# Attention kernel: one transposed tile moves to the scores' PSUM banks, gate tiles alternate between two banks, and gate products wait for their sums one by one

## The chip, the core and the metric

The kernel runs on one core of one Trainium2 chip. The metric is the device time of one execution in microseconds (us); the median of several executions is compared. In the profile PE is TensorE, DVE is VectorE, ACT is ScalarE, POOL is GpSimd and SP is SyncE, which issues the DMAs.

## The reference, cut to what matters

The first block mixes a sequence of 512 rows by two linear-attention mixers and merges them under gates. The part that matters here is the second mixer's gate, `sigmoid(mg + b_gate)`: one 1024 x 1024 matmul on the 512 rows. Then come two hybrid layers. Each computes, for four blocks of 128 queries, causal attention of four kinds: selected keys ("slc"), window ("win"), latent ("mla") and a short window of 128 keys ("swa"), and a small attention on compressed keys, whose result is added to the same output as slc and win:

```
p_c = softmax(where(valid_c, lc, NEG)) * valid_c        # 128 queries x 4 heads x up to 31 compressed keys
o_cmp = einsum(p_c, vc)
o = g0 * o_cmp + g1 * o_slc + g2 * o_win
mixed = concatenate([o, o_b, o_c]) * silu(z)            # z = h @ w_in[..., ZC:], the layer's output gate
x = x + rms_norm(mixed @ w_out, g_post)
```

## The kernel before

Every engine has its own program, written in the order in which it runs; semaphores join them. Each engine counts what it has finished; a name such as `nt["g7", p, k]` or `ng["gS", p]` is the count to wait for, and a later count covers all earlier ones. A wait for a count that was already waited for is left out.

**PSUM.** There are eight banks of 512 columns. `ps.take(t, name, bank=b)` lets PE wait until whoever read the bank's last tile is done (`ps.empty`). Without `bank` the banks go round.

**The second mixer's gate** (`yb_t`, `seven_gates_t`). The 1024 x 1024 matmul is cut in four parts p; each is done by seven half-size products, in the manner of Strassen, instead of eight. Their operands are sums of blocks: POOL makes four sums of weights for each p (`seven_sums_g`, line 1900), DVE makes four sums of rows once (`seven_sums_v`, line 1890). One product is four matmuls of 256 columns in the program and eight records in the profile (every float32 matmul of the program shows as two). PE takes the tiles (p, k) in the order (0,0), (1,0), (0,1), (0,2), (0,3), (1,1), ... `G7` says which products a tile holds: k=0 products 1 and 2, which need no sum; k=1 products 6 and 7; k=2 products 5 and 3; k=3 product 4. Ahead of every k>0 PE waits for all four sums of weights of that p and all four sums of rows.

**Attention** (`attn_t`). The 40 jobs (ten per block of queries, each a kind and two heads, e=0 and 1) run through a pipeline: in round i PE makes the scores of job i, transposes the weights of job i-4 (`turn`, line 2688), and multiplies job i-6 by the values (`product`). DVE adds the bias and finds the least score (`least`, line 2794); ACT exponentiates (line 2916); DVE takes reciprocals (line 2800); POOL scales (lines 2973 and 2975); PE transposes; DVE (line 2781) and ACT (line 2926) share the copies out of PSUM. In even rounds PE goes transposes, gate, scores, products; in odd rounds products, scores, gate, transposes. DVE's copy of a transposed tile stands behind `least` of the same round in odd rounds.

Banks: scores go round `rings[0]`, transposed tiles round `rings[1]`. Until round 12 (`few`) these are banks (0,1) and (3,4), and banks 2 and 5 hold the tiles of the layer's output gate; later (`all_`) they are (2,0,1) and (5,3,4). In round 5 of each block of queries `turn_cmp` transposes the compressed weights (line 2697) into a bank of `rings[1]`, and DVE copies it (line 2822).

**The output gate** z (`out_gate`): six of its eight tiles m are spread over rounds 0 to 11, four matmuls of 512 columns per round, in the order 5, 4, 0, 1, 2, 3, in bank `(2, 5)[m % 2]`. When a tile is full ACT takes its tanh (line 2438) and DVE multiplies it (line 2433), which empties the bank.

Of the kernel before, what the change touches and what calls it, by code (L numbers as in the profile page):

```python
# [8 lines left out]
ALU = mybir.AluOpType  # L9
# [103 lines left out]
def program(nc, I, out):  # L113
# [3 lines left out]
    sv, sa, sg, st = (nc.alloc_semaphore(f"{e}_finished") for e in ("vector", "scalar", "gpsimd", "tensor"))  # L117
    nv, na, ng, nt = Count(), Count(), Count(), Count()
# [25 lines left out]
    ps = Banks(nc.alloc_psum_tensor("PS", [128, 4096], F32))  # L144

    def mm(t, o, l, r, s, p):
        return t.matmul(o, l, r, start=s, stop=p, skip_group_check=True)  # L147
# [27 lines left out]
    def weights(t, k):  # L175

        t.wait_ge(s_ring[ring_slot(k)], 16 * sum(wparts(i) for i in range(k + 1) if ring_slot(i) == ring_slot(k)))
        return wviews(k)
# [1630 lines left out]
    def yb_t(t):  # L1809
        meet(t, "delta")  # L1810
        seven_gates_t(t)
        t.wait_ge(sv, nv["y", "b"])
        for h in range(4):
            p = ps.take(t, "yT", "b", h)
            for a in range(4):
                for c in range(2):
                    x = t.go.transpose(p[:, 128 * a + 64 * c:128 * a + 64 * c + 64],
                                       sqB[rows(h), 512 * a + 256 * (h // 2) + 128 * c:512 * a + 256 * (h // 2) + 128 * c + 128],
                                       ident[rows(h), rows(h)])
            x.then_inc(st, nt("yT", "b", h))  # L1820
        nt.mark("at", "yb")

    def yb_v(v):
        meet(v, "delta")
        seven_sums_v(v)
        head_norm_v(v, oB, sqB, s4B, "b")
        nv.mark("y", "b")
        for p in range(4):
            seven_gates_v(v, p)
        for h in range(4):  # L1830
            v.wait_ge(sa, na["bg", h])
            v.wait_ge(st, nt["yT", "b", h])
            v.do.scalar_tensor_tensor(out=ybT[:, h, :], in0=ps["yT", "b", h][:, :], scalar=vc("gon"), in1=gateB[h],
                                      op0=ALU.mult, op1=ALU.mult).then_inc(sv, nv("ybT", h))
            ps.empty(sv, nv, "yT", "b", h)
        nv.mark("at", "yb")
# [15 lines left out]
    def yb_g(g):  # L1852
        meet(g, "delta")
        for p in range(2):
            seven_sums_g(g, p)
        rsq_g(g, s4B, "heads", "b")
        for p in range(2, 4):
            seven_sums_g(g, p)
        ng.mark("at", "yb")
# [15 lines left out]
    T1g, T2g, T4g = (AR[:, VT_at + 1024 * i:VT_at + 1024 * i + 1024].rearrange("p (k n) -> p k n", k=4) for i in range(3))  # L1875
# [3 lines left out]
    he, hf, hg, hh = (hT[:, 4 * (i // 2):4 * (i // 2) + 4, 256 * (i % 2):256 * (i % 2) + 256] for i in range(4))  # L1879

    def gate_blocks(w, p):
        return [w[:, 4 * (i % 2):4 * (i % 2) + 4, 256 * (p % 2) + 128 * (i // 2):256 * (p % 2) + 128 * (i // 2) + 128] for i in range(4)]

    def gate_sums(p):
        return [AR[:, ST_at[p % 3] + 512 * i:ST_at[p % 3] + 512 * i + 512].rearrange("p (k n) -> p k n", k=4) for i in range(3)]

    def seven_sums_v(v):

        for o, x, y in ((T1g, hf, he), (T2g, hh, T1g), (hf, hh, hf), (T4g, hg, T2g)):
            v.do.tensor_tensor(o, x, y, ALU.subtract).then_inc(sv, nv("gT"))  # L1890

    def seven_sums_g(g, p):

        w, = weights(g, 13 + 2 * (p // 2))
        a, b, c, d = gate_blocks(w, p)
        s1, s2, s4_ = gate_sums(p)
        if p == 3:
            g.wait_ge(st, nt["g7", 0, 3])
        for o, x, y, op in ((s1, c, d, ALU.add), (s2, s1, a, ALU.subtract), (c, a, c, ALU.subtract), (s4_, b, s2, ALU.subtract)):
            g.do.tensor_tensor(o, x, y, op).then_inc(sg, ng("gS", p))  # L1900


    G7 = ((1, 2), (6, 7), (5, 3), (4,))

    def seven_gates_t(t):
        for p, k in [(0, 0), (1, 0)] + [(p, k) for p in range(2) for k in range(1, 4)] + [(p, k) for p in range(2, 4) for k in range(4)]:
            w, = weights(t, 13 + 2 * (p // 2))
            a, b, c, d = gate_blocks(w, p)
            s1, s2, s4_ = gate_sums(p)
            if k:  # L1910
                t.wait_ge(sg, ng["gS", p])
                t.wait_ge(sv, nv["gT"])
            o = ps.take(t, "g7", p, k)
            for i, what in enumerate(G7[k]):
                left, right = {1: (a, he), 2: (b, hg), 3: (s4_, hh), 4: (d, T4g), 5: (s1, T1g), 6: (s2, T2g), 7: (c, hf)}[what]
                for q in range(4):
                    x = mm(t.go, o[:, 256 * i:256 * i + 256], left[:, q, :], right[:, q, :], q == 0, q == 3)
            x.then_inc(st, nt("g7", p, k))
            if p % 2 and k == 3:
                nt.mark("weights", 13 + 2 * (p // 2))  # L1920
# [390 lines left out]
    def two_t(t, l):  # L2311
# [95 lines left out]
        for i in range(8):  # L2407
            out_gate(t, l, 7, i)
# [6 lines left out]
        for i in range(8):  # L2415
            out_gate(t, l, 6, i)

    def out_gate(t, l, m, i, bank=None):

        k = W2 + 10 * l + 7 - m // 4  # L2420
        w, = weights(t, k)
        if i == 0:
            ps.take(t, "sz", l, m, bank=bank)
        x = mm(t.go, ps["sz", l, m][:, :], w[:, i, 128 * (m % 4):128 * (m % 4) + 128], hT2[:, i, :], i == 0, i == 7)
        if i == 7:
            x.then_inc(st, nt("sz", l, m))
            if m in (4, 3):
                nt.mark("weights", k)

    def out_gate_v(v, l, m):  # L2430
# [170 lines left out]
    NJ, PER = len(JOBS), 10  # L2601
    TURN, PV = 4, 6
    CMP_EXP, CMP_SUM, CMP_TURN, CMP_PV = 1, 2, 5, {1: 0, 4: 1}
    GATES = [(m, i) for m in (5, 4, 0, 1, 2, 3) for i in range(8)]
    PER_JOB = 4
    FILLED = len(GATES) // PER_JOB

    def gates_in(i):

        x = GATES[PER_JOB * i:PER_JOB * i + PER_JOB]  # L2610
        return x, [m for m, k in x if k == 7]
# [39 lines left out]
    def attn_t(t, l):  # L2651
# [41 lines left out]

        def turn_cmp(qb):
            t.wait_ge(sg, ng["pc", l, qb])
            p = ps.take(t, "pcT", l, qb, bank=next(rings[1]))
            t.go.transpose(p[:, 0:128], Pc.rearrange("p h c -> p (h c)"), ident).then_inc(st, nt("pcT", l, qb))

        def product(j):
# [24 lines left out]
        def turned(i):  # L2724
            qb, at = divmod(i, PER)
            if TURN <= i < NJ + TURN:
                turn(i - TURN)
            if qb < 4 and at == CMP_TURN:
                turn_cmp(qb)
# [15 lines left out]
        def filled(i):  # L2745
            for m, k in gates_in(i)[0]:
                out_gate(t, l, m, k, bank=(2, 5)[m % 2])

        for i in range(NJ + PV):
            rings = few if i <= FILLED else all_  # L2750
# [377 lines left out]
```

## Time and profile before

| | |
|---|---|
| median of 3 runs | 1378.41 us (1377.52 to 1380.28) |
| the profiled execution | 1377.88 us, of which 1376.1 us span |
| PE busy | 1310.5 us, 95% |
| DVE, ACT, POOL busy | 46%, 30%, 26% |
| gate of the second mixer | 600 to 651 us |
| attention of the two layers | 865 to 1003 us, 1180 to 1318 us |

The span runs from the first instruction to the last; about 1.8 us of the execution lie around it. A timeline row is: start, duration, engine, line, operation, shapes, number of records merged, and in brackets the idle time of the engine just before the row and what ended it.

### The profile page before, as it was taken

The numbers are of one execution on the slowest core, as the hardware profiler recorded it, in microseconds if no ns is written. First come the engines' busy times: TensorE is split into PE (matmuls) and PEld (weight loads), VectorE is DVE, ScalarE is ACT, GpSimd is POOL, SyncE is SP. The second block draws the span as 40 slices with busy tenths as digits, with TensorE's granted clock in tenths as the row PEclk, the third lists the DMA queues.
The fourth block names the chain that finished last, engine by engine and source line by source line (L and its number), as shares of the span: only waits on it lengthen the run. The fifth ranks groups of instructions, "written<-read, shape, count | busy, mean of one in ns | idle before, by whom it ended". The sixth has DMA issues, their size and how long they took to land.

```text
span 1376.1 us, 23425 instructions
## 1 busy us (share of the span) xinstructions
PE 1310.5 (95%) x9443; PEld 763.7 (55%) x9443; DVE 637.9 (46%) x1350; ACT 416.8 (30%) x901; POOL 354.6 (26%) x437
## 2 busy tenths in 40 slices
PE   5999989999999999999999999998999999998897
PEld 3454654555566677668445645445655645445553
DVE  4266627747233344464464222237636131327735
ACT  4233303353432222201015112236613212236621
POOL 0100000112323443153430000127631000117631
PEclk9999999999999999999999999999999999999999
DMA  9611012011220100032244315110003515100001
GB/s 318 251 61 62 2 63 77 8 53 62 77 110 3 64 2 3 3 122 75 100 158 105 117 31 184 62 50 1 2 16 74 148 31 183 62 1 1 1 1 61
DMA packets 71530, 96.52 MB, mean 70 GB/s; under 512 B 27639, under 2 KB 35247, under 8 KB 71422
## 3 DMA queue, kind: packets, MB, share of 16 engines
q1 hardware_dynamic: 71050, 94.76, 20.5%
q8 instruction: 74, 1.21, 0.4%
q10 hardware_dynamic: 372, 0.27, 0.1%
q14 instruction: 34, 0.28, 0.1%
HBM read 92.89 MB, written 2.13 MB: 69 GB/s over the span
## 4 chain that ended last, share of the span: by engine, by line
PE 85%; DVE 7%; ACT 2%; issue 2%; SPq 2%; POOL 1%; DMA 1%; DVEq 0%; POOLq 0%; ACTq 0%
PE PS L147 82%; PE PS L2688 2%; DVE AR L2794 2%; DMA AR<-in_w_mod 1%; SPq L187 1%; DVE AR L2781 1%; POOL AR L1900 1%; ACT AR L2916 1%; DVE AR L2045 0%; PE PS L1383 0%; SPq L304 0%; PE PS L2103 0%; DVE AR L819 0%; ACT AR L2926 0%; DVE AR L2830 0%
## 5 line engine op out<-in xcount | busy, mean ns | idle before, releaser
L147 PE MATMUL PS<-AR 64*64 64x64 f32 (+14 forms) x8806 | 1236.5, 337 | 36.8 <-ACT AR L2926 6.6
L147 PEld LDWEIGHTS PS<-AR 64*64 64x64 f32 (+5 forms) x8806 | 694.0, 155 | 551.3 <-issue 462.5
L2916 ACT ACTIVATE AR<-AR 128x257 f32<-128x257 f32 (+5 forms) x160 | 84.9, 530 | 104.8 <-DVE AR L2794 95.5
L2794 DVE CUSTOM_DVE_ANT_0 AR<-PS,AR 128x257 f32<-128x257 f32 (+5 forms) x160 | 72.3, 452 | 67.1 <-PE PS L147 50.0
L412 POOL TENSOR_TENSOR AR<-AR 128x1 f32<-128x1 f32 (+4 forms) x26 | 21.8, 840 | 280.4 <-DVE AR L407 233.6
L1175 DVE SCALAR_TENSOR_TENSOR AR<-AR 128x441 f32<-128x441 f32 (+2 forms) x96 | 78.6, 819 | 19.6 <-ACT AR L1132 15.9
L1557 DVE TENSOR_TENSOR AR<-PS,AR 128x256 f32<-128x256 f32 x60 | 25.5, 425 | 100.7 <-PE PS L147 97.7
L2975 POOL TENSOR_SCALAR AR<-AR 128x257 f32<-128x257 f32 (+5 forms) x96 | 53.4, 556 | 62.2 <-DVE AR L2800 54.8
L2688 PE MATMUL PS<-AR 128*128 128x128 f32 x352 | 51.2, 283 | 8.4 <-DVE AR L2781 6.3
L1684 ACT ACTIVATE AR<-PS 128x512 f32<-128x512 f32 x48 | 28.7, 598 | 92.5 <-PE PS L147 90.0
L2973 POOL TENSOR_SCALAR AR<-AR 128x128 f32<-128x128 f32 (+3 forms) x64 | 38.9, 608 | 66.5 <-DVE AR L2800 61.7
L1992 POOL TENSOR_TENSOR AR<-AR 128x512 f32<-128x512 f32 x36 | 47.5, 1319 | 31.4 <-DMA AR<-in_w_o 28.4
L2688 PEld LDWEIGHTS PS<-AR 128*128 128x128 f32 x352 | 39.0, 143 | 29.4 <-issue 14.1
L2045 DVE TENSOR_TENSOR AR<-PS,AR 128x512 f32<-128x512 f32 x40 | 27.7, 692 | 52.4 <-PE PS L147 50.7
L1792 POOL TENSOR_TENSOR AR<-AR 128x512 f32<-128x512 f32 x20 | 21.0, 1050 | 84.2 <-PE PS L147 55.6
L2926 ACT ACTIVATE AR<-PS 128x512 f32<-128x512 f32 (+2 forms) x56 | 30.1, 537 | 28.6 <-PE PS L2688 24.7
L2433 DVE SCALAR_TENSOR_TENSOR AR<-AR,PS 128x512 f32<-128x512 f32 x16 | 11.0, 688 | 52.1 <-ACT AR L2438 52.0
L2781 DVE COPY AR<-PS 128x512 f32<-128x512 f32 (+2 forms) x48 | 28.9, 602 | 7.9 <-PE PS L2688 6.4
L2983 POOL TENSOR_TENSOR AR<-AR 128x28 f32<-128x28 f32 (+3 forms) x8 | 2.5, 315 | 112.3 <-DVE AR L2810 111.8
L2000 POOL TENSOR_TENSOR AR<-AR 128x512 f32<-128x512 f32 x12 | 16.9, 1407 | 55.0 <-PE PS L147 54.3
L1195 POOL TENSOR_TENSOR AR<-AR 128x512 f32<-128x512 f32 (+1 forms) x12 | 12.9, 1071 | 68.5 <-ACT AR L1141 50.3
L1900 POOL TENSOR_TENSOR AR<-AR 128x512 f32<-128x512 f32 x16 | 27.2, 1700 | 11.4 <-DVE AR L1627 10.1
(260 smaller groups left out, 880.5 us busy)
## 6 DMA issues: line engine op xcount, KB each, us to landing
AR<-in_w_in SPq DMA_DIRECT2D x16, 2048.0 KB, 8.8
AR<-in_w_mod SPq DMA_DIRECT2D x6, 2048.0 KB, 12.8
AR<-in_w_out SPq DMA_DIRECT2D x4, 2048.0 KB, 12.9
AR<-in_x SPq DMA_DIRECT2D x8, 512.0 KB, 5.9
AR<-in_w_in SPq DMA_DIRECT2D x4, 1024.0 KB, 7.8
AR<-in_w_o SPq DMA_DIRECT2D x2, 2048.0 KB, 8.5
AR<-in_w_in SPq DMA_DIRECT2D x2, 1664.0 KB, 9.4
AR<-in_w_in SPq DMA_DIRECT2D x12, 256.0 KB, 4.8
```

Source lines behind the costliest of these rows:

```text
L147: return t.matmul(o, l, r, start=s, stop=p, skip_group_check=True)
L1175: v.do.scalar_tensor_tensor(out=o_, in0=xi[:, r0 + i - 1:r1 + i - 1, c0 + c - 1:c1 + c - 1], scalar=tap(i, c), in1=o_, op0=ALU.mult, op1=A ...
L1684: a_.do.activation(XX[n], ps.two("xx", n, k_, k)[:, new_at(k):new_at(k) + 512], ACT.Copy, bias=0.0, scale=1.0).then_inc(sa, na("xx", n, k_ ...
L1900: g.do.tensor_tensor(o, x, y, op).then_inc(sg, ng("gS", p))
L1992: g.do.tensor_tensor(o, x, y, ALU.subtract).then_inc(sg, ng(*name, "T"))
L2688: x = t.go.transpose(p[:, c + 128 * b:c + 128 * b + 128], PB[j % NJP][e][:, at[b]:at[b] + 128], ident)
L2781: write(dst, src).then_inc(sem, count("pT", l, j, e))
L2794: v.do.tensor_tensor_reduce(PB[j % NJP][e][:, 0:nk], ps["s", l, j, e][:, 0:nk], bias_for(qb, kind, 2 * a + e, nk), 1.0, 3e38, ALU.add, ALU ...
L2916: a_.do.activation(P, P, ACT.Exp, bias=mn[:, j % NJS, e:e + 1], scale=-1.0, accum_out=su[:, j % NJS, e:e + 1]).then_inc(sa, na("p", l, j, e))
L2926: out_of_psum(a_, sa, na, lambda o, x: a_.do.activation(o, x, ACT.Copy, bias=0.0, scale=1.0), l, i - TURN, e)
L2973: x = g.do.tensor_scalar(P, P, r, gt_[:, qb, c:c + 1], ALU.mult, ALU.mult)
L2975: x = g.do.tensor_scalar(P, P, r, one_c, ALU.mult, ALU.mult)
```

## The change

Three edits. (1) In the second mixer's gate each product waits for the one sum that it reads (`G7_S`, `G7_T`), no longer for all eight. (2) The output gate's tiles go in the order 5, 4, 1, 0, 3, 2, so that neighbouring tiles have different banks; the release of the weights' ring slot moves to the tile that is now last. (3) For blocks of queries 1 to 3 the transposed compressed weights take a bank of the scores' ring; the ring of the transposed tiles is not advanced there, so the tile after it gets the bank one place earlier in that ring, and the scores after it one place later in theirs.

```diff
     def seven_sums_v(v):
-        for o, x, y in ((T1g, hf, he), (T2g, hh, T1g), (hf, hh, hf), (T4g, hg, T2g)):
-            v.do.tensor_tensor(o, x, y, ALU.subtract).then_inc(sv, nv("gT"))
+        for i, o, x, y in ((1, T1g, hf, he), (2, T2g, hh, T1g), (3, hf, hh, hf), (4, T4g, hg, T2g)):
+            v.do.tensor_tensor(o, x, y, ALU.subtract).then_inc(sv, nv("gT", i))
...
-            g.do.tensor_tensor(o, x, y, op).then_inc(sg, ng("gS", p))
+            g.do.tensor_tensor(o, x, y, op).then_inc(sg, ng("gS", p, i))
...
+    G7_S, G7_T = {5: 1, 6: 2, 7: 3, 3: 4}, {5: 1, 6: 2, 7: 3, 3: 3, 4: 4}
...
-            if k:
-                t.wait_ge(sg, ng["gS", p])
-                t.wait_ge(sv, nv["gT"])
             o = ps.take(t, "g7", p, k)
             for i, what in enumerate(G7[k]):
+                if what in G7_S:
+                    t.wait_ge(sg, ng["gS", p, G7_S[what]])
+                if what in G7_T:
+                    t.wait_ge(sv, nv["gT", G7_T[what]])
...
-            if m in (4, 3):
+            if m in (4, 2):
                 nt.mark("weights", k)
...
-    GATES = [(m, i) for m in (5, 4, 0, 1, 2, 3) for i in range(8)]
+    GATES = [(m, i) for m in (5, 4, 1, 0, 3, 2) for i in range(8)]
...
-            p = ps.take(t, "pcT", l, qb, bank=next(rings[1]))
+            p = ps.take(t, "pcT", l, qb, bank=next(rings[0] if qb else rings[1]))
```

No instruction is added or removed, and the orders of DVE, ACT, POOL and SP stay as they were; only PE's waits change. In the pieces below, "vector_finished" is a wait for DVE, "gpsimd_finished" for POOL, "scalar_finished" for ACT, "ring..._landed" for a DMA of weights.

PE in the second mixer's gate; the row with x15 ends the tiles (0,0) and (1,0), and the row after it opens (0,1):

```order
 L147 MATMUL PS<-AR 128x256 x15
 L147 MATMUL PS<-AR 128x256 [waits vector_finished,gpsimd_finished]
-L147 MATMUL PS<-AR 128x256 x19
+L147 MATMUL PS<-AR 128x256 x3
+L147 MATMUL PS<-AR 128x256 [waits vector_finished,gpsimd_finished]
+L147 MATMUL PS<-AR 128x256 x7
 L147 MATMUL PS<-AR 128x256 [waits gpsimd_finished]
-L147 MATMUL PS<-AR 128x256 x19
+L147 MATMUL PS<-AR 128x256 x3
+L147 MATMUL PS<-AR 128x256 [waits vector_finished]
```

The one wait ahead of twenty matmuls became waits ahead of single products. Over the whole stage, from (0,1) to the last product, 7 matmuls with a wait became 16.

PE in round 4 of a layer's attention: two transposes of job 0, four matmuls of the third gate tile (128x512), then the scores of job 4 (128x128, two rows):

```order
-L2688 MATMUL PS<-AR 128x128 [waits gpsimd_finished] x2
-L147 MATMUL PS<-AR 128x512 [waits vector_finished,ring1_landed]
-L147 MATMUL PS<-AR 128x512 x3
-L147 MATMUL PS<-AR 128x128 x2
+L2691 MATMUL PS<-AR 128x128 [waits gpsimd_finished] x2
+L147 MATMUL PS<-AR 128x512 [waits ring1_landed]
+L147 MATMUL PS<-AR 128x512 x3
+L147 MATMUL PS<-AR 128x128 [waits vector_finished] x2
```

The gate tile lost its wait for DVE; the scores of job 4 now show a wait for DVE of their own, which the gate tile's had covered.

PE in rounds 35 and 36, last block of queries: the compressed weights (first row, line 2697, 2700 after), the four transposes of job 32, the two scores of job 36 (128x512):

```order
-L2697 MATMUL PS<-AR 128x128 [waits scalar_finished,gpsimd_finished]
-L2688 MATMUL PS<-AR 128x128 [waits vector_finished]
-L2688 MATMUL PS<-AR 128x128 x3
-L147 MATMUL PS<-AR 128x512 x2
+L2700 MATMUL PS<-AR 128x128 [waits vector_finished,gpsimd_finished]
+L2691 MATMUL PS<-AR 128x128 [waits scalar_finished]
+L2691 MATMUL PS<-AR 128x128 x3
+L147 MATMUL PS<-AR 128x512 [waits vector_finished] x2
```

The transposes wait for ACT in place of DVE, and the compressed weights and the scores have a wait for DVE that they lacked. Round 25 and 26 (third block) change in the same way. In the second block the compressed weights and the first score after them gain a wait for DVE, and nothing is lost.

## Rows read from the trace of the kernel before

**Rows 1.** The page, part 1: busy time, share of the span, instructions of each engine.

```profile
PE 1310.5 (95%) x9443; PEld 763.7 (55%) x9443; DVE 637.9 (46%) x1350; ACT 416.8 (30%) x901; POOL 354.6 (26%) x437
```

**Rows 2.** Timeline, 596 to 634 us, the second mixer's gate.

```profile
600.11 7.68 DVE L1890 TENSOR_TENSOR AR<-AR 128x1024 f32<-128x1024 f32 x4
...
600.13 7.18 PE L147 MATMUL PS<-AR 128*128 128x256 f32 x32 [0.79 <-DVE AR L1627]
600.16 15.91 POOL L1900 TENSOR_TENSOR AR<-AR 128x512 f32<-128x512 f32 x8 [10.13 <-DVE AR L1627]
...
608.97 25.36 PE L147 MATMUL PS<-AR 128*128 128x256 f32 x116 [1.65 <-POOL AR L1900]
...
619.25 12.46 POOL L1900 TENSOR_TENSOR AR<-AR 128x512 f32<-128x512 f32 x8
621.57 6.88 DVE L1925 TENSOR_TENSOR AR<-PS,AR 128x256 f32<-128x256 f32 x14
```

**Rows 3.** Critical chain, 590 to 665 us: start, duration, what; POOL's third and fourth sum.

```profile
604.58 2.14 POOL AR L1900
...
606.79 2.13 POOL AR L1900
```

**Rows 4.** DVE's line 1890: min/median/max in ns, first and last start in us.

```profile
L1890 DVE TENSOR_TENSOR AR<-AR x4: 1226/2086/2179, 600.1 to 605.6; 128x1024 f32<-128x1024 f32 x4
```

**Rows 5.** Groups by line and form, PE, 617 to 619 us: count, busy us, mean ns, idle.

```profile
L147 PE MATMUL PS<-AR 128*128 128x256 f32 x11 | 2.5, 378 | 0.0
```

**Rows 6.** Four windows of line 147, 608.97 to 650.70 us: total length, then PE busy.

```profile
sum 41.73, PE 41.73 PEld 36.18; mean PE 10.43 PEld 9.04
```

**Rows 7.** Timeline, 876 to 894 us: round 4 of the first layer.

```profile
881.27 0.69 DVE L2433 SCALAR_TENSOR_TENSOR AR<-AR,PS 128x512 f32<-128x512 f32 x1 [2.79 <-ACT AR L2438]
...
882.11 4.10 PE L147 MATMUL PS<-AR 128*128 128x512 f32 x12 [1.28 <-DVE AR L2433]
```

**Rows 8.** Timeline of PE, second layer, round 4.

```profile
1197.03 4.10 PE L147 MATMUL PS<-AR 128*128 128x512 f32 x12 [1.28 <-DVE AR L2433]
```

**Rows 9.** Timeline, first layer, rounds 25 to 27.

```profile
955.28 0.43 DVE L2794 CUSTOM_DVE_ANT_0 AR<-PS,AR 128x257 f32<-128x257 f32 x1
...
956.36 0.66 PE L2688 MATMUL PS<-AR 128*128 128x128 f32 x4 [0.28 <-DVE AR L2781]
...
960.86 0.42 DVE L2794 CUSTOM_DVE_ANT_0 AR<-PS,AR 128x257 f32<-128x257 f32 x1 [0.75 <-PE PS L147]
```

**Rows 10.** Timelines of PE and of DVE, second layer, rounds 26 and 27.

```profile
1271.62 0.66 PE L2688 MATMUL PS<-AR 128*128 128x128 f32 x4 [0.62 <-DVE AR L2781]
...
1276.13 0.42 DVE L2794 CUSTOM_DVE_ANT_0 AR<-PS,AR 128x257 f32<-128x257 f32 x1 [0.76 <-PE PS L147]
```

**Rows 11.** Timeline, first layer, rounds 35 to 37.

```profile
983.40 0.42 DVE L2794 CUSTOM_DVE_ANT_0 AR<-PS,AR 128x257 f32<-128x257 f32 x1
...
983.87 0.69 DVE L2781 COPY AR<-PS 128x512 f32<-128x512 f32 x1
...
984.61 0.66 PE L2688 MATMUL PS<-AR 128*128 128x128 f32 x4 [1.59 <-DVE AR L2781]
984.66 0.29 DVE L2822 COPY AR<-PS 128x128 f32<-128x128 f32 x1
...
985.11 4.85 PE L147 MATMUL PS<-AR 96*128 96x512 f32 x42
...
989.99 0.42 DVE L2794 CUSTOM_DVE_ANT_0 AR<-PS,AR 128x257 f32<-128x257 f32 x1 [1.35 <-PE PS L147]
```

**Rows 12.** Timelines of PE and of DVE, second layer, rounds 36 and 37.

```profile
1299.88 0.66 PE L2688 MATMUL PS<-AR 128*128 128x128 f32 x4 [1.60 <-DVE AR L2781]
...
1305.26 0.42 DVE L2794 CUSTOM_DVE_ANT_0 AR<-PS,AR 128x257 f32<-128x257 f32 x1 [1.30 <-PE PS L147]
```

**Rows 13.** Timeline of POOL, first layer, round 13 on.

```profile
926.07 1.21 POOL L2973 TENSOR_SCALAR AR<-AR 128x256 f32<-128x256 f32 x2 [5.65 <-DVE AR L2800]
```

**Rows 14.** Windows of 5 us: busy by engine, granted clock, DMA share, GB/s.

```profile
930.00:935.00 5.00, 5.00 (x34) 3.88 (x32) 4.05 (x14) 2.52 (x9) 3.14 (x5) 0.73 0.00 0
```

More of the change, by code:

```diff
@@ L1898, in seven_sums_g @@
             g.wait_ge(st, nt["g7", 0, 3])
-        for o, x, y, op in ((s1, c, d, ALU.add), (s2, s1, a, ALU.subtract), (c, a, c, ALU.subtract), (s4_, b, s2, ALU.subtract)):
-            g.do.tensor_tensor(o, x, y, op).then_inc(sg, ng("gS", p))
+        for i, o, x, y, op in ((1, s1, c, d, ALU.add), (2, s2, s1, a, ALU.subtract), (3, c, a, c, ALU.subtract), (4, s4_, b, s2, ALU.subtract)):
+            g.do.tensor_tensor(o, x, y, op).then_inc(sg, ng("gS", p, i))
     G7 = ((1, 2), (6, 7), (5, 3), (4,))
+    G7_S, G7_T = {5: 1, 6: 2, 7: 3, 3: 4}, {5: 1, 6: 2, 7: 3, 3: 3, 4: 4}
     def seven_gates_t(t):
```

## The prediction

> **What bounds the kernel now.** I read the page first: PE is busy for 1310.5 of 1376.1 us [rows 1], so time can only come from the 65 us in which PE idles, or from work taken off it; the change takes none off. Then I read the timeline at the three places that the diff touches, looking at the bracket ahead of each PE row: how long PE stood, and which line let it go. Last I looked at what DVE and POOL did at the same moment, since a stall that goes is worth only what the next engine in the chain can follow.
>
> **Gate of the second mixer.** PE makes the tiles (0,0) and (1,0) from 600.13 to 607.31, stands for 1.65 us and goes on at 608.97, released by POOL's line 1900 [rows 2]. The chain shows why: POOL's fourth sum runs from 606.79 to 608.92 [rows 3], and PE waits for all four. Product 6, the next one, reads only the second sum of each kind. POOL's was done when its third began at 604.58 [rows 3]. DVE's four end at 607.79 [rows 2], and none takes less than 1.226 us [rows 4], so its second was done by 605.34. So product 6 can start at 607.31.
>
> The later products must not be early. PE's 116 records take 25.36 us, 0.219 us each [rows 2], so a product of eight takes 1.75 us. Product 7 is due at 609.06; POOL's third sum is done at 606.72 [rows 3] and all of DVE's at 607.79. Product 3 is due at 612.56, its sum is there at 608.92. The tile (1,1) is due at 616.06, and by 616.07 POOL has done all eight sums of the first two parts [rows 2]; it needs the sixth. The third part starts at 624.8: its bank was emptied by DVE's first line 1925, which begins at 621.57, and its second sum is needed at 628.3, while POOL runs the last eight sums from 619.25 to 631.71 [rows 2], 1.56 us each, so it is there near 622.4. The last part needs sums from 640.5 on. No new stall, then.
>
> What a stall costs is more than its bracket: in a row without idle time records last 0.378 us [rows 5] and follow each other every 0.219 us, so they overlap by 0.16 us, which a stall loses. Term: 1.65 + 0.16 = 1.81 us. I take the same 0.16 us for the other places (an estimate from these rows).
>
> The price of the waits themselves: 9 more matmuls carry one. The seven before cost nothing that can be seen: in 41.73 us that hold six of them PE is busy for 41.73 us [rows 6]. So I take zero. If each emptied PE's overlap, the bound is 9 x 0.16 = 1.44 us. The Trainium skill (Advanced Engine Details and Errata, Network/Comms) puts reading a semaphore from a sequencer at 50 to 100 ns; nine such reads in PE's path would be an estimated 0.45 to 0.9 us, and the sum below would be 7.8 to 7.3 us in place of 8.2. The trace disagrees for the waits that it has, if they are met in time.
>
> **Output gate.** In round 4 of each layer PE stands for 1.28 us [rows 7, 8], because tile 0 wants bank 2, which tile 4 has just filled and DVE's line 2433 empties from 881.27 to 881.96 [rows 7]. With tile 1 next the bank is 5, whose last tile was finished two rounds earlier. The scores behind it wait for `least` of round 3, which stands ahead of line 2433 on DVE, so that is no new stall. Tiles 0, 3 and 2 then find a bank that was filled two rounds before, as tiles 1 to 3 did until now. Does the gain last? POOL idles for 5.65 us until 926.07 [rows 13] waiting for DVE, and DVE's least score waits for PE, so all engines move with PE. Term: 2 x (1.28 + 0.16) = 2.88 us. Bounds: 0 if a later wait takes it, 2.88 us.
>
> **Compressed weights.** The transposes of job 22 wait 0.28 us in the first layer [rows 9] and 0.62 in the second [rows 10], those of job 32 wait 1.59 [rows 11] and 1.60 [rows 12], all for DVE's copy (line 2781) of the tile that had their bank, which on DVE stands behind `least` of the same round. With the shorter ring order they want a bank that ACT emptied a round before; that stall goes. What is late next? The scores of job 36 now need both banks of job 35's. Without the stall the transposes start at 983.02 and the scores at 983.5 (985.11 - 1.59) [rows 11]. `least` leaves the second bank at 983.82 [rows 11], and the second score comes one score later, at 984.4 (512 columns, twice the 0.44 us that 256 take [rows 2]): 0.5 us to spare. The first bank is free earlier still. In round 26 the scores start at 956.6 and the later bank is free at 955.71 [rows 9]. So nothing new on PE. But DVE does not move: it runs through from the copy at 983.87 and next waits for PE, 1.35 us before 989.99 [rows 11] and 1.30 before 1305.26 [rows 12]. That idle time is all that it can give, less 0.10, the distance that DVE keeps when PE is long done (983.87 + 0.69 to 984.66) [rows 11]. The same cap in the second layer's round 27 is 0.76 - 0.10 [rows 10]; in the first layer 0.75 [rows 9] does not bind. Terms: 0.28 + 0.16 = 0.44; 0.66; 1.25; 1.20. Together 3.55 us. Bounds: 0 if each goes into the next wait; without DVE's cap 0.44 + 0.78 + 1.75 + 1.76 = 4.73.
>
> In the second block the added wait is for scores two places back; I take zero, bounded by one wait of the size of 0.28 us in each layer.
>
> **Sum.** 1.81 + 2.88 + 3.55 = 8.24 us. Against the profiled execution, 1377.88, that is 1369.6; the median of the runs is 0.53 above that execution, so I forecast 1370.2, 0.6% faster. A measurement of this kernel tells about 0.2% (2.8 us) from no change.
>
> **Rivals**, on the scale of the median.
>
> *The compressed weights' gain goes into the next wait* (3.55 us lost): 1373.7. For it: DVE has no idle time until 988.6. Against: the 1.35 us right behind.
>
> *The added waits cost PE its overlap*: 1.44 us, 1371.6.
>
> *TensorE's clock falls once or twice more.* In 930 to 935 us the granted clock is 0.73 of full speed [rows 14], so 1.2 GHz for 2.7 of these 5 us and 2.4 GHz for the rest, after short stalls and small matmuls; that loses 1.35 us of full-speed work. Twice where PE is the bound: 1372.9. For it: the stretches are full of short matmuls and short waits, and the change moves where they fall. Against: it takes idle time out. The Trainium skill (TensorE: Matmul & The Clock Gate, A second HAM failure mode) says that going round PSUM banks with small idle gaps between groups of matmuls lets the clock fall again and again; by that rule alternating banks would lose what the waits gave. The trace bears it out at one place in the two layers' attention [rows 14].
>
> *The scores' ring runs short; slower.* Each of the six transposes of compressed weights (three blocks, two layers) takes one of three score banks until DVE's copy. If PE reached the scores before DVE had emptied the banks, each place would cost the old stall plus that copy: 1.59 + 0.10 + 0.29 = 1.98 us [rows 11], 11.9 in all. Against it stand 4.69 us from the two gates and the four stalls removed, 4.09: 3.1 us slower, 1381.5. It decides when the spare 0.5 us above is gone. That bank is held for about one round and `least` precedes the copy on DVE, so I hold it unlikely.
>
> *The waits do not fall away*, because another release comes just as late: 1378.4. Each bracket names the releaser, and the three found are those that the diff removes.
>
> **Chances.** Forecast 0.68; next wait 0.12; added waits 0.06; clock 0.08; ring short 0.03; nothing 0.03. The first four are faster by more than 0.2%: 0.94, of which I give 0.02 to what I have not seen: faster 0.92, same 0.05, slower 0.03. The range reaches down to the sum without DVE's cap (9.42 us, 1369.0) and 1.8 us under it for the spread of the runs, and up to the case 1373.7 with 0.5 added: 1367.2 to 1374.2.
>
> **What will show it.** Right: no bracket of POOL's line 1900 ahead of PE near 607 us; none of line 2433 in round 4; none of line 2781 ahead of the transposes right after line 2697; the idle time of DVE in rounds 27 and 37 near its minimum; the first three gains still there at the span's end. Wrong: brackets of DVE's line 2794 or 2822 ahead of the scores of rounds 16, 17, 26, 27, 36 and 37, gaps at each waiting product in the gate, or new windows with a clock under 1.

## The result, and the profile after

The changed kernel takes 1369.78 us (median of 4 runs, 1369.23 to 1372.44) where the kernel before takes 1378.51 (4 runs, 1377.52 to 1380.28): a ratio of 0.9941, with a 95% interval of 0.9925 to 0.9957. Measured once more beside other runs of before, it was 1371.12 against 1379.76, 0.9938 (0.9924 to 0.9952). The forecast was 1370.2, so 0.9940.

The changed kernel's lines stand three further down in its file from the gate on (line 2794 is 2797, 2781 is 2784, 2688 is 2691, 2697 is 2700). Its page begins:

```profile
span 1370.6 us, 23430 instructions
...
PE 1312.6 (96%) x9443; PEld 766.5 (56%) x9443; DVE 636.6 (46%) x1350; ACT 416.5 (30%) x901; POOL 354.8 (26%) x437
```

The span is 5.5 us shorter, the median 8.7. The difference is time that this execution lost before it came to anything that was changed: it reached the gate at 603.11 us, the kernel before at 600.13 [rows 2]. So I compare stretches. These are the windows of the gate, from its first matmul to the transposes behind it, of the changed kernel and then of the kernel before (length, PE busy, weight loads, DVE, ACT, POOL, granted clock, DMA share, GB/s):

```profile
603.11:651.75 48.64, 48.64 (x225) 42.22 (x225) 27.01 (x35) 6.12 (x11) 30.13 (x17) 1.00 0.33 123
```
```profile
600.13:650.70 50.57, 48.91 (x225) 42.15 (x225) 27.02 (x35) 6.12 (x11) 30.11 (x17) 1.00 0.31 118
```

PE now has no idle time in the gate, and the stretch is 1.93 us shorter: the idle 1.65 us [rows 2], and 0.27 us by which PE is busy longer with the same records (48.91 against 48.64), because the stall breaks their overlap. The timeline of round 4 in the first layer of the changed kernel, on PE (the bracket is the idle time ahead of a row and the line that ended it; where a row has none, PE did not stand):

```profile
881.50 0.38 PE L2691 MATMUL PS<-AR 128*128 128x128 f32 x2
881.72 4.03 PE L147 MATMUL PS<-AR 128*128 128x512 f32 x12
886.13 4.14 PE L147 MATMUL PS<-AR 64*128 64x129 f32 x11 [0.39 <-DVE AR L2797]
```

The bracket of 1.28 us [rows 7] is gone, and the scores of round 5 come 4.63 us after round 4's transposes; in the kernel before these are at 880.44 and 886.59, 6.15 apart. The gain is 1.52 us, and 1.51 in the second layer, where the bracket is gone as well. The timeline of rounds 36 and 37 in the first layer, PE and then DVE:

```profile
981.79 0.27 PE L2700 MATMUL PS<-AR 128*128 128x128 f32 x1
981.90 0.60 PE L2691 MATMUL PS<-AR 128*128 128x128 f32 x4
982.36 4.96 PE L147 MATMUL PS<-AR 96*128 96x512 f32 x42
...
989.71 0.63 PE L2691 MATMUL PS<-AR 128*128 128x128 f32 x4 [0.93 <-DVE AR L2784]
```
```profile
982.92 0.69 DVE L2784 COPY AR<-PS 128x512 f32<-128x512 f32 x1
983.71 0.29 DVE L2825 COPY AR<-PS 128x128 f32<-128x128 f32 x1
...
987.52 0.17 DVE L2803 RECIPROCAL AR<-AR 128x2 f32<-128x2 f32 x1
987.83 0.42 DVE L2797 CUSTOM_DVE_ANT_0 AR<-PS,AR 128x257 f32<-128x257 f32 x1
```

The transposes no longer wait after the turned weights (1.59 us [rows 11]). By the scores behind them PE has won 1.79 us: they start 0.57 us after the turned weights, where it was 985.11 - 982.75 = 2.36. But 7.35 us after those scores PE stands for 0.93 us, for DVE's copy, where before it stood 0.45 there. What stays is 1.20 us: from the turned weights to those transposes 7.92 us, before 9.12 (982.75 to 991.87). DVE shows why: its wait of 1.35 us [rows 11] has shrunk to the 0.14 us between 987.69 and 987.83, the distance it also keeps ahead of `least` where it does not wait (977.25 to 977.39 in the kernel before). DVE now sets the pace of this place, as the cap in the prediction said. The second layer's rounds 26 and 27 on PE, in the changed kernel:

```profile
1267.00 0.33 PE L2700 MATMUL PS<-AR 128*128 128x128 f32 x1 [0.87 <-POOL AR L2989]
1267.17 0.60 PE L2691 MATMUL PS<-AR 128*128 128x128 f32 x4
...
1273.61 0.52 PE L2691 MATMUL PS<-AR 128*128 128x128 f32 x3 [0.88 <-DVE AR L2784]
```

The 0.62 us [rows 10] are gone. From the turned weights to the bracketed transposes it is 6.61 us, before 7.21 (1270.67 to 1277.88): 0.60 won. The same distance won 0.49 us in the first layer's rounds 26 and 27, and 1.16 in the second layer's 36 and 37.

From the first gate matmul to the end of the last matmul of the program it is 759.85 us (603.11 to 1362.96); in the kernel before, 768.27 (600.13 to 1368.40). That is 8.42 us, and the pieces named above add to 8.41.

### The profile page after: what moved, and what is told of

Same layout as the page of the kernel before. It is cut to its first block, busy times and chain, and to the rows that moved or that the text cites. A ratio compares the mean times of both kernels' runs of the same rounds, so it can differ in the third digit from the quotient of the medians.

```text
span 1370.6 us, 23430 instructions
## 1 busy us (share of the span) xinstructions
PE 1312.6 (96%) x9443; PEld 766.5 (56%) x9443; DVE 636.6 (46%) x1350; ACT 416.5 (30%) x901; POOL 354.8 (26%) x437
## 4 chain that ended last, share of the span: by engine, by line
PE 87%; DVE 5%; POOL 3%; ACT 2%; issue 2%; DMA 1%; ACTq 0%; DVEq 0%; POOLq 0%
PE PS L147 83%; PE PS L2691 2%; POOL AR L2978 1%; DVE AR L2797 1%; POOL AR L1995 1%; ACT AR L2919 1%; DMA AR<-in_onehot 1%; PE PS L353 0%; DVE AR L2048 0%; POOL AR L2976 0%; DVE AR L2784 0%; PE PS L1383 0%; ACT AR L2929 0%; PE PS L2106 0%; DVE AR L819 0%
```

## The experiments

The theory is that of the prediction: each stall is worth its bracket and a little lost overlap, the waits themselves cost nothing, and DVE's idle time caps the compressed weights' gain. The rivals are those of the prediction too. The whole time of one execution is a blunt measure here, since the stretch ahead of the gate, which no kernel changes, ended anywhere from 599.7 to 605.9 us. So each experiment was read by the ratio over its runs and by the stretch from the first gate matmul to the end of the last matmul in its profile:

| kernel | median us | ratio to before (95%) | stretch us | less than 768.27 |
|---|---|---|---|---|
| gate alone | 1378.58 | 0.9992 (0.9978 to 1.0005) | 768.03 | 0.24 |
| tile order alone | 1376.77 | 0.9971 (0.9961 to 0.9981) | 766.87 | 1.40 |
| banks alone | 1377.06 | 0.9973 (0.9965 to 0.9981) | 765.34 | 2.93 |
| turned weights alone | 1376.58 | 0.9970 (0.9957 to 0.9982) | 764.88 | 3.39 |
| changed, 72 more waits | 1371.44 | 0.9940 (0.9927 to 0.9954) | 759.92 | 8.35 |
| changed, bank held | 1373.58 | 0.9961 (0.9948 to 0.9975) | 763.48 | 4.79 |
| changed, copies on ACT | 1368.93 | 0.9925 (0.9912 to 0.9938) | 758.78 | 9.49 |
| changed, POOL earlier | 1368.89 | 0.9925 (0.9912 to 0.9938) | 757.64 | 10.63 |
| changed, both of these | 1366.43 | 0.9905 (0.9888 to 0.9921) | 754.68 | 13.59 |
| changed, again | 1371.12 | 0.9938 (0.9924 to 0.9952) | 759.80 | 8.47 |
| before, again | 1381.19 | one run | 768.36 | -0.09 |

**The gate alone**, on the kernel before: the numbered sums and the waits at each product, nothing else.

```diff
-            if k:
-                t.wait_ge(sg, ng["gS", p])
-                t.wait_ge(sv, nv["gT"])
...
+                if what in G7_S:
+                    t.wait_ge(sg, ng["gS", p, G7_S[what]])
+                if what in G7_T:
+                    t.wait_ge(sv, nv["gT", G7_T[what]])
```

> Only the gate's waits are changed (edit 1), on the kernel before. Theory (three separate local gains): no bracket ahead of PE near the start of the tile (0,1); the stretch from the first gate matmul to the first transpose behind the gate (50.56 us before, 600.13 to 650.70) becomes 48.65 us, 1.9 us shorter, and the time falls by 1.8 to 1.9 us. Rival (added waits cost PE its overlap): only 0.4 us shorter. Rival (a later stage takes it back): the stretch is shorter, the span is not.

Its timeline on PE has the gate in one piece, 605.94 to 654.58, the same 48.64 us as in the changed kernel:

```profile
605.94 48.71 PE L147 MATMUL PS<-AR 128*128 128x256 f32 x224 [0.79 <-DVE AR L1627]
654.58 0.59 PE L1817 MATMUL PS<-AR 64*128 64x64 f32 x7
```

So the edit gives its 1.93 us alone. The whole stretch gained only 0.24, because at another place this execution lost 1.59: the 34 matmuls that begin at 1276.10 took 5.57 us in place of 3.98, at a granted clock that fell. Two of its windows there:

```profile
1276.00:1278.00 2.00, 2.00 (x9) 0.89 (x9) 1.74 (x4) 0.29 (x1) 1.65 (x4) 0.78 0.00 0
1278.00:1280.00 2.00, 2.00 (x22) 2.00 (x22) 1.11 (x5) 1.42 (x4) 1.74 (x2) 0.50 0.00 0
```

Here 0.50 of full speed is 1.2 GHz. The ratio's interval takes in both a gain of 1.9 us (0.9986) and no change; by itself it settles nothing.

**The order of the gate tiles alone**, and **the banks alone**, with the old order, but each tile in the other bank than the tile ahead of it.

```diff
-            if m in (4, 3):
+            if m in (4, 2):
...
-    GATES = [(m, i) for m in (5, 4, 0, 1, 2, 3) for i in range(8)]
+    GATES = [(m, i) for m in (5, 4, 1, 0, 3, 2) for i in range(8)]
```

> Only the order of the output gate's tiles is changed (edit 2), on the kernel before. Theory: the bracket of 1.28 us ahead of the third tile is gone in both layers, the distance from the transposes of round 4 to the scores of round 5 (6.15 us before, 880.44 to 886.59) becomes 4.6 us, and the time falls by 2.9 to 3.0 us. Rival (POOL or DVE is the bound in the next rounds and takes it back): the time falls by less than 1 us.

```diff
-                out_gate(t, l, m, k, bank=(2, 5)[m % 2])
+                out_gate(t, l, m, k, bank=5 if m in (5, 0, 2) else 2)
```

> The order of the tiles stays as before (5, 4, 0, 1, 2, 3); only their banks are made to alternate: 5, 2, 5, 2, 5, 2. Theory (the stall is the bank alone): the same 2.9 to 3.0 us as with the order changed. Rival (it matters which tile and which weights come third): a bracket stays ahead of the third tile and the time falls by under 1 us.

Round 4 in the first layer on PE, with the order changed and then with the banks changed:

```profile
880.66 0.38 PE L2688 MATMUL PS<-AR 128*128 128x128 f32 x2
880.87 4.03 PE L147 MATMUL PS<-AR 128*128 128x512 f32 x12
885.29 4.57 PE L147 MATMUL PS<-AR 64*128 64x129 f32 x12 [0.39 <-DVE AR L2794]
```
```profile
882.51 0.38 PE L2688 MATMUL PS<-AR 128*128 128x128 f32 x2
882.72 4.03 PE L147 MATMUL PS<-AR 128*128 128x512 f32 x12
887.14 4.57 PE L147 MATMUL PS<-AR 64*128 64x129 f32 x12 [0.39 <-DVE AR L2794]
```

Both make it 4.63 us, 1.52 less than before. So the gain is the bank's distance of two rounds and not which tile is made when. The first of the two executions again met the fall of the clock in the second layer (5.59 us for the 34 matmuls); with that 1.61 added its stretch gained 3.01, the other's 2.93.

**The turned weights alone.**

```diff
-            p = ps.take(t, "pcT", l, qb, bank=next(rings[1]))
+            p = ps.take(t, "pcT", l, qb, bank=next(rings[0] if qb else rings[1]))
```

> Only the bank of the transposed compressed weights is changed (edit 3), on the kernel before. Theory: the brackets of line 2781 ahead of the transposes that follow the compressed weights are gone in blocks 3 and 4; DVE's idle time behind falls from 0.75 and 1.35 us to near its minimum; the time falls by 3.3 to 3.6 us. Rival (PE's gain is not capped by DVE): 4.7 us. Rival (the scores' ring runs short): brackets ahead of the scores of rounds 16, 26 and 36, and less than 1 us gained or a loss.

The stretch is 3.39 us shorter. Corrected for the falls of the clock, the three edits alone give 1.83 + 3.01 + 3.39 = 8.23 us; together they gave 8.42. The gains add to within 0.2 us, so none of the three lived off another's stall.

**72 more waits.** In the changed kernel, every matmul of the gate's last three parts waits for a count that POOL reached before the stage began: 88 matmuls of the gate with a wait instead of 16.

```diff
                 for q in range(4):
+                    if p:
+                        t.go.wait_ge(sg, ng["at", "delta"])
                     x = mm(t.go, o[:, 256 * i:256 * i + 256], left[:, q, :], right[:, q, :], q == 0, q == 3)
```

> The changed kernel, with a further wait ahead of each of the 84 matmuls of parts 1 to 3 of the second mixer's gate, for a count that POOL reached before the stage began: 88 matmuls with a wait in place of 16. Theory (a wait that is already met costs PE nothing): the stretch from the first gate matmul to the first transpose behind it stays at 48.6 us. Rival (each costs the 0.16 us of overlap): 72 x 0.16 = 11.5 us longer, 60 us.

Its window of the gate:

```profile
602.29:650.93 48.64, 48.64 (x225) 42.22 (x225) 27.01 (x35) 6.12 (x11) 30.15 (x17) 1.00 0.32 123
```

It is 48.64 us, to the hundredth what it is without them. At 0.16 us each, as in the rival, 72 waits would have made it 60.2. The Trainium skill (Advanced Engine Details and Errata, Network/Comms) gives 50 to 100 ns for a semaphore read; this trace shows nothing of it in PE's path for a wait that is met in time.

**The bank held longer.** In the changed kernel, DVE copies the turned weights out one round later, so that the scores' ring is one bank short for longer. The copy is also what the compressed product reads, two rounds after the turned weights.

```diff
-            if qb < 4 and at == CMP_TURN:
+            if qb < 4 and at == CMP_TURN + 1:
```

> The changed kernel, with DVE's copy of the transposed compressed weights one round later (round 6 of each block in place of round 5), so that the scores' bank is held longer. Theory (the bank came back just in time, with some half a microsecond to spare): the first score two rounds later now waits for that copy, and the kernel loses 0.3 to 1 us at each of six places, 2 to 6 us in all, so most or all of what edit 3 gave. Rival (the scores' ring has ample room): no change within 0.2%.

A wait for line 2825 (2822 of before) appears in every block. Here it is on PE in round 7 and round 37 of the first layer, and in round 37 of the second:

```profile
893.30 4.55 PE L147 MATMUL PS<-AR 128*128 128x128 f32 x14 [0.35 <-DVE AR L2825]
...
985.07 1.12 PE L147 MATMUL PS<-AR 128*128 128x128 f32 x6 [1.14 <-DVE AR L2825]
...
1298.87 1.12 PE L147 MATMUL PS<-AR 128*128 128x128 f32 x6 [1.49 <-DVE AR L2825]
```

It takes back 3.63 us of the stretch, a size that was expected, but not by the expected wait. The bracket stands ahead of the compressed product (`product_cmp`, 128*128), which reads the copy; the scores (64*128) come behind it, at 985.49. In round 7, in the first block, the turned weights keep a bank of the other ring, and the same wait stands there, 0.35 us in both layers. So this run shows what a late copy costs the product that reads it. What a short ring would cost it does not show, since the scores behind would have had to wait for the same copy.

For the ring the changed kernel itself has the answer. No wait for line 2825 stands ahead of PE in its attention, and in blocks 2 to 4 the copy ends 2.1 to 2.9 us before the scores that take its bank (984.00 and 986.61 in the first layer's last block).

**The copies of jobs 22 and 32 on ACT.** If DVE is the cap, taking two copies from it must give back what PE lost 7 us later.

```diff
-        return j % 2 == 0 if e == "both" else e == 0
+        return j % 2 == 0 and j not in (22, 32) if e == "both" else e == 0
```

> The changed kernel, with the copies of jobs 22 and 32 out of PSUM made by ACT in place of DVE (0.69 us each off DVE at the place where DVE, not PE, set the gain). Theory (DVE caps edit 3): the least scores of rounds 36 and 37 come some 0.7 us sooner, the bracket of 0.93 us ahead of the transposes of job 34 falls to 0.4, and the kernel gains 0.4 to 0.6 us at each of the two places of block 4 and up to 0.2 in block 3: about 1.2 us. Rival (DVE is not the cap): no gain, or a loss of up to 0.6 us where ACT becomes late.

The first layer's rounds 36 and 37 on PE:

```profile
981.36 0.27 PE L2700 MATMUL PS<-AR 128*128 128x128 f32 x1
...
988.79 0.63 PE L2691 MATMUL PS<-AR 128*128 128x128 f32 x4 [0.45 <-DVE AR L2784]
```

The distance is 7.43 us against 7.92, and the bracket is back at 0.45. Then PE keeps 1.69 us of the 1.79 that it won, where the cap of the changed kernel left 1.20. The stretch is 1.07 us shorter than the changed kernel's, near the 1.2 expected.

**POOL's order.** The wait ahead of the turned weights, 0.87 us for line 2989 (2986 in the kernel before, where it stands too), is POOL's. In this kernel POOL does another scaling five rounds earlier, and has no sum of weights in round 22: the later sums each come one even round later, the last in round 38.

```diff
-            if i == 15:
+            if i == 10:
                 g.wait_ge(s_pst, 16 * (l + 1))
...
-            if 14 <= i < 38 and i % 2 == 0:
+            if 14 <= i < 40 and i % 2 == 0 and i != 22:
...
-                sums_of_weights(g, w0 + 8, w0 + 9, ("y2", l), (i - 14) // 2)
+                sums_of_weights(g, w0 + 8, w0 + 9, ("y2", l), (i - 14) // 2 - (i > 22))
```

> The changed kernel, with POOL's work moved: the scaling of the 1024-wide norm row (2.78 us) from round 15 to round 10, and the sum of output weights of round 22 to round 38. Theory (PE's brackets for POOL, 0.47, 0.21 and 0.87 us in each layer, are POOL's queue and not its data): these brackets go, and the kernel gains 1 to 3 us in the two layers together; where DVE or ACT is next, less. Rival (another engine bounds those rounds): the brackets change their releaser and nothing is gained.

The first layer's rounds 26 and 27 on PE:

```profile
951.37 0.27 PE L2700 MATMUL PS<-AR 128*128 128x128 f32 x1
...
951.91 4.61 PE L147 MATMUL PS<-AR 96*128 96x384 f32 x34
...
958.64 0.52 PE L2691 MATMUL PS<-AR 128*128 128x128 f32 x3 [0.98 <-DVE AR L2784]
```

The bracket of 0.87 is gone, the stretch 2.21 us shorter than the changed kernel's, although the 34 matmuls took 4.61 us here and 4.69 in the second layer, in place of 3.98; and DVE is late next, 0.98 us.

The longer row is not the clock, which was 1.00 in both (951.91 to 956.52 and 1262 to 1268). Its last four matmuls are the scores of round 27, two for each head. In the repeated changed kernel the two heads' matmuls start together (957.33 and 957.34). Here the second head's start 0.62 us after the first's, and 0.06 us after DVE has finished the first `least` of round 26, in both layers. DVE and then PE in the first layer:

```profile
955.21 0.56 DVE L2797 CUSTOM_DVE_ANT_0 AR<-PS,AR 128x384 f32<-128x384 f32 x1
955.69 0.08 DVE L2797 DVE_READ_ACCUMULATOR2_ANT AR<- 128x1 f32 x1
...
955.83 0.48 PE L147 MATMUL PS<-AR 64*128 64x257 f32 x1
```

So the next bound is DVE here too. No bracket shows it, because PE was busy with the first head's matmuls.

**Both, beside the changed kernel and the kernel before once more.** The diff is that of the last two together.

> The copies of jobs 22 and 32 on ACT together with POOL's earlier scaling and moved sum. From the first turned compressed weights of layer 1 to the last matmul the changed kernel takes 472.21 us, with ACT's copies alone 471.11 (1.10 less), with POOL's order alone 469.77 (2.44 less). Theory: the two remove different waits (DVE's behind line 2784, POOL's ahead of line 2700), so the gains add to 3.5 us or somewhat more, since in the run with POOL's order PE then stood 0.98 us for DVE in round 27, which is the idle time that ACT's copies shorten: a stretch near 468.5, ratio to the kernel before near 0.991. Rival: ACT, which now copies in the rounds in which PE already waits 0.5 to 0.7 us for its line 2929, becomes late, and the gain stays at that of POOL's order: a stretch near 469.8, ratio 0.9925.

> The changed kernel once more, beside the one above and in as many rounds, so that both stand against the same runs of the kernel before: ratio 0.994, within 0.0015. Its profile shows whether the 2.98 us that the first profiled execution was late at the second mixer's gate belong to the change: if they do, the first gate matmul starts near 603.1 again; if they are a matter of the execution (the clock in the first 250 us), anywhere from 598 to 606, and from the first gate matmul to the last matmul of the program it takes 759.9 us again, give or take 1.5.

> The kernel before once more, for one more profile. In the runs of the gate alone and of the tiles alone, which keep the stall of 0.6 us ahead of the transposes after line 2697 in layer 2's round 26, the clock fell right behind it and the 34 matmuls there took 5.6 us in place of 3.98; no profile of a kernel without that stall showed it. If the stall is what lets the clock fall, it can be seen here (in two of four profiles so far); if it is a matter of the execution alone, it says nothing either way, and from the first gate matmul to the last matmul it takes 768.3 us, give or take 1.6.

The three reach the gate at 603.60, 601.31 and 603.34 us. The first rows of the gate of the changed kernel and of the kernel before, both repeated:

```profile
601.31 8.92 PE L147 MATMUL PS<-AR 128*128 128x256 f32 x40 [0.79 <-DVE AR L1627]
```
```profile
603.34 6.97 PE L147 MATMUL PS<-AR 128*128 128x256 f32 x31 [0.79 <-DVE AR L1627]
```

The order has turned round: now the kernel before is the later one, by 2.0 us. So the 2.98 us of the first profile are the execution's and not the change's. The stretches repeat to 0.1 us: 759.80 and 768.36. The kernel before had no fall of the clock behind its stall in the second layer (3.98 us).

Both together take 754.68 us, 5.17 less than the changed kernel, more than the 1.07 and 2.21 alone. From the first turned weights to the last matmul it is 467.1 us, where 468.5 was expected. Of the 1.9 us that the two do not give alone, 1.2 are the scores of round 27, which start together here (the 34 matmuls take 4.00 and 4.08 us): the copy of job 22, which in POOL's run kept DVE 0.69 us ahead of `least`, is ACT's here. Of the other 0.7 us, 0.3 lie ahead of the first layer's attention and 0.4 in rounds 5 to 27. Its ratio of 0.9905 against 0.9938 beside the same runs of before, with intervals that do not touch, makes it the best version: 0.95% under the kernel before.

## Why the prediction was right

**Which stalls fall away, and what bounds.** The signs of "right" are in the trace: no bracket of POOL's sums in the gate, none of the gate copy in round 4, none ahead of the transposes behind the turned weights, DVE's idle time in both rounds 37 and in the second layer's round 27 at its minimum. (In the first layer's round 27, where the cap was not to bind, 0.26 us of it are left.) The gains are still there at the end of the last matmul.

**The terms.** Predicted and measured by distances in the two profiles: gate 1.81 and 1.93; output gate 2.88 and 3.03; compressed weights 0.44, 0.66, 1.25, 1.20 and 0.49, 0.60, 1.20, 1.16. The sum was 8.24, and 8.41 came. Two sizes were a little off. What a stall loses beside its bracket was taken as 0.16 us, from the length and spacing of the records; measured it is 0.28 in the gate (1.93 - 1.65) and 0.24 in round 4 (1.52 - 1.28). Most of the difference is the first matmul behind the stall, shown here with the next two of the kernel before:

```profile
608.97 0.48 PE L147 MATMUL PS<-AR 128*128 128x256 f32 x1 [1.65 <-POOL AR L1900]
609.29 0.60 PE L147 MATMUL PS<-AR 128*128 128x256 f32 x2
```

The next matmul starts 0.32 us after it, where in a row without idle time it is 0.22: 0.10 us that the prediction had not counted. In round 4 the same distance is 0.50 in place of 0.43 us. The other size is DVE's: it kept 0.14 us and not 0.10 where it is the cap. The prediction took the distance between two copies, and the cap stands ahead of `least`.

The two sizes err in opposite ways, 0.27 us too little for the gates and 0.10 too much for the compressed weights, so the sum is nearer than its terms. That the median came within 0.5 us of the forecast is luck in part: the ratio's interval is 4.4 us wide.

**The next wait takes the gain.** It took part of it, 0.59 us of 1.79 in the first layer's last block, exactly where DVE's idle time ran out, and the cap had it in the sum; without the cap the four terms would have been 4.73, and 3.45 came. The copies on ACT show that it is DVE: they take 0.48 us out of that wait.

**The added waits cost overlap.** Refuted by the 72 waits, for waits that are met in time.

**The ring runs short.** One of the signs named for "wrong" did appear, in round 16 of the second layer, where the added wait now holds the scores for line 2797; the same row stands in the first layer of the repeated run. These are PE's rows of the changed kernel:

```profile
1242.22 1.87 PE L147 MATMUL PS<-AR 96*128 96x256 f32 x12 [0.36 <-DVE AR L2797]
1244.25 1.95 PE L147 MATMUL PS<-AR 128*64 128x128 f32 x14 [0.15 <-ACT AR L2929]
```

The kernel before has no wait at the first place and 0.73 us at the second. From the turned weights to the row after these it is 4.97 us (1241.16 to 1246.13) and 4.96 before (1244.83 to 1249.79). The new wait comes out of the one behind it, which had to be waited for in any case. The zero in the sum was right; the sign was not one of harm by itself. The other sign, a wait for the copy of the turned weights, did not appear, so no run shows the 11.9 us that the prediction set on it. In round 36 no margin was left on the first bank, which the prediction took to be free earlier still: the first score starts 0.06 us after `least` has left it (982.30 and 982.36 in the first layer).

**A wait that the prediction did not look for.** The output gate's last tile is now tile 2, in bank 2, which the scores take next; before it was tile 3, in bank 5. So the scores behind the gate tiles wait for line 2436 (2433 before), in both layers, and also with the tile order alone and with the banks alone. PE in the first layer, before and after:

```profile
921.80 1.92 PE L147 MATMUL PS<-AR 64*128 64x257 f32 x14
924.52 0.70 PE L147 MATMUL PS<-AR 64*128 64x256 f32 x2 [0.79 <-DVE AR L2794]
```
```profile
923.02 0.70 PE L147 MATMUL PS<-AR 64*128 64x256 f32 x2 [0.38 <-DVE AR L2436]
924.05 0.70 PE L147 MATMUL PS<-AR 64*128 64x256 f32 x2 [0.34 <-DVE AR L2797]
```

It comes out of the 0.79 us that PE waited there before: from the first turned weights to the second of these two scores it is 33.30 us in both (891.22 to 924.52, 890.75 to 924.05). It costs nothing here, but it was not on the prediction's list.

**The clock falls.** At the place of [rows 14] the changed kernel's window shows a clock of 0.81 in place of 0.73:

```profile
930.00:935.00 5.00, 5.00 (x37) 3.92 (x36) 3.99 (x14) 2.95 (x9) 3.10 (x5) 0.81 0.00 0
```

What it loses there PE doesn't lose at the end: from the first turned weights to those of round 26 it takes 64.54 us (890.75 to 955.29), in the kernel before 64.53, and 64.57 in the repeated kernel before (894.51 to 959.08), whose clock did not fall. PE waits for others right behind it. In the changed kernel's second layer, without a fall, it stands 0.36 and 0.15 us for DVE and ACT in round 16 (the rows above), in the first, with the fall, for neither, and the wait for POOL that comes next ends equally late, 48.86 and 48.87 us after the first turned weights:

```profile
939.61 0.44 PE L2691 MATMUL PS<-AR 128*128 128x128 f32 x2 [0.47 <-POOL AR L2978]
...
1251.33 0.44 PE L2691 MATMUL PS<-AR 128*128 128x128 f32 x2 [0.51 <-POOL AR L2978]
```

Such a fall stands at this place, in one or both layers, in six of the thirteen profiles: the kernel before, the changed one, the turned weights alone, the 72 waits, the copies on ACT and POOL's order. Each began before the turned weights of the second block, the first that edit 3 moves in a layer.

The Trainium skill (TensorE: Matmul & The Clock Gate, A second HAM failure mode) warns of a clock that falls again and again where groups of matmuls go round banks with short idle times between them; the tiles in alternating banks show none of it, and the window 880 to 887 has a clock of 1.00. What remains of this rival is one place, the 34 matmuls behind the turned weights of the second layer's round 26: the clock fell there in two of the thirteen profiles, the gate alone and the tile order alone, both times behind the stall that the change removes. Five profiles have that stall and eight do not, so whether removing it also steadies the clock stays open.

## What to carry to other kernels

A stall on the bound engine is worth its bracket plus a broken overlap and a longer first matmul (here 0.24 to 0.28 us together), but only as far as the idle time of the next engine in the chain reaches; read that engine's bracket a few us later and cap the term by it. A counting semaphore that marks each product by itself, and a wait at each consumer, cost nothing here where the waits are met in time, so wait for what is needed and not for the group. When a gain is under 1% of a long program, compare the distance between two milestones of the trace: it repeated to 0.1 us here, while whole executions of one kernel spread over 3 us and more. Look first for falls of the clock inside it, which took up to 1.61 us. And when an experiment makes a wait appear, look which instruction stands behind the bracket: a late copy can hold the one that reads it and not the one that wants its bank.

## What was not expected of the hardware

Ahead of the gate all kernels run the same instructions, yet reach it from 599.68 us (with the bank held) to 605.94 (the gate alone). The spread of 6.3 us, three quarters of the gain of the change, arises in the first 250 us: the same matmul record, the 1501st, starts anywhere from 246.48 to 252.81, and from 250 us to the gate the granted clock is 1.00. The first matmul already starts anywhere from 9.39 to 11.94. Of the windows of 50 us there, 150 to 200 us has the lowest clock in every profile. Its rows in the kernel before, with the gate alone and with the tile order alone, which came to the gate at 600.13, 605.94 and 600.41:

```profile
150.00:200.00 50.00, 44.10 (x569) 28.39 (x569) 22.62 (x51) 10.59 (x21) 0.00 (x0) 0.92 0.12 44
```
```profile
150.00:200.00 50.00, 44.08 (x606) 29.45 (x610) 19.97 (x50) 9.60 (x19) 0.00 (x0) 0.86 0.12 44
```
```profile
150.00:200.00 50.00, 45.58 (x569) 30.54 (x568) 20.66 (x51) 10.60 (x21) 0.00 (x0) 0.86 0.12 44
```

A clock of 0.86 in place of 0.92 went with the latest arrival, and in the third row with an early one, in which PE idled 1.5 us less. What makes one execution early there and another late was not found.
